# Latent attention: both heads' gate products in front of the next pair's query rotation on VectorE

## The reference

```
q = einsum('bsr,rhd->bshd', q_c, w_uq)          # 128 plain + 64 rotary features a head
q_rope = apply_rope(q[..., 128:], cos, sin)
q_lat = einsum('bshd,rhd->bshr', q[..., :128], w_uk)
s = q_lat . kv_c + q_rope . k_rope              # times ATTN_SCALE, masked by chunks of 64
o_lat = softmax(s) . kv_c
o = einsum('bshr,rhd->bshd', o_lat, w_uv)
return (o * silu(z)) @ w_out                    # z: the gate, 2048 features of the input projection
```

## Time and profile before

| | us |
| --- | --- |
| median of 3 runs | 2120.88 |
| lowest and highest run | 2120.36, 2125.22 |
| span of the profiled execution, first to last instruction | 2123.0 |
| PE busy | 1988.0 |
| DVE busy | 1021.4 |
| ACT busy | 852.1 |
| POOL busy | 797.5 |
| stretch of the eight pairs of heads, about | 1704 to 2015 |

### The profile page before, as it was taken

One profiled execution on the slowest core, in us unless ns is written; L12 is line 12 of the kernel. 1 busy time (PEld: TensorE's weight loads), 2 busy tenths in 40 slices (PEclk: granted clock), 3 DMA queues, 4 the chain that ended last, 5 costly groups with the idle time before them and its releaser, 6 DMA issues.

```text
span 2123.0 us, 29194 instructions
## 1 busy us (share of the span) xinstructions
PE 1988.0 (94%) x9640; PEld 1642.4 (77%) x9640; DVE 1021.4 (48%) x2371; ACT 852.1 (40%) x1566; POOL 797.5 (38%) x368
## 2 busy tenths in 40 slices
PE   7889999999999899999999998999999889999896
PEld 5778788888778788878888886877887567777684
DVE  5483765421254767546553216657312664444414
ACT  4463422222343676542222224222223465555523
POOL 3323454444454100126444442545444223242340
PEclk9889999999999899999999999999999989999999
DMA  7432455422333112126553322322322112121121
GB/s 244 127 92 67 150 178 164 138 92 96 99 110 121 36 45 66 42 79 199 176 168 99 99 95 74 106 92 95 99 93 95 43 57 69 40 69 49 60 79 40
DMA packets 70011, 209.40 MB, mean 99 GB/s; under 512 B 9739, under 2 KB 15115, under 8 KB 69948
## 3 DMA queue, kind: packets, MB, share of 16 engines
q1 hardware_dynamic: 57724, 174.72, 25.7%
q10 hardware_dynamic: 12224, 33.85, 5.0%
HBM read 196.90 MB, written 8.49 MB: 97 GB/s over the span
## 4 chain that ended last, share of the span: by engine, by line
PE 58%; issue 21%; DVE 9%; POOL 9%; ACT 2%; DVEq 0%; POOLq 0%; ACTq 0%
PE bank L938 15%; PE bank L939 15%; PE bank L940 15%; POOL wsp L442 9%; PE bank L1215 3%; PE bank L1362 1%; PE bank L1199 1%; PE bank L1381 1%; PE bank L1188 1%; PE bank L1084 1%; PE bank L1373 1%; PE bank L1211 1%; PE bank L972 1%; PE bank L1061 1%; DVE gen L1614 0%
## 5 line engine op out<-in xcount | busy, mean ns | idle before, releaser
L442 POOL TENSOR_TENSOR wsp<-raw,wsp 128x1024 fp32r<-128x1024 f32 x294 | 730.6, 2490 | 1047.9 <-ACT wsp L515 1047.7
L938 PE MATMUL bank<-xs,wsp 128*128 128x512 f32 x1320 | 525.9, 398 | 36.0 <-DVE mid L2040 16.0
L939 PE MATMUL bank<-xs,wsp 128*128 128x512 f32 x1320 | 519.1, 393 | 0.0
L940 PE MATMUL bank<-xs,wsp 128*128 128x512 f32 x1320 | 518.9, 393 | 0.0
L515 ACT ACTIVATE wsp<-raw 128x1024 fp32r<-128x1024 f32 x294 | 307.3, 1052 | 234.4 <-PE bank L940 205.6
L938 PEld LDWEIGHTS bank<-xs,wsp 128*128 128x128 f32 x1320 | 251.3, 190 | 97.0 <-issue 32.3
L938 PE MATMUL bank<-xk,wsp 128*128 128x512 f32 x752 | 295.4, 393 | 9.5 <-DVE xk L1482 5.1
L939 PE MATMUL bank<-xk,wsp 128*128 128x512 f32 x752 | 294.5, 392 | 0.0
L940 PE MATMUL bank<-xk,wsp 128*128 128x512 f32 x752 | 294.4, 391 | 0.0
L940 PEld LDWEIGHTS bank<-xs,wsp 128*128 128x128 f32 x1320 | 250.8, 190 | 53.6
L939 PEld LDWEIGHTS bank<-xs,wsp 128*128 128x128 f32 x1320 | 251.4, 190 | 52.1 <-issue 1.4
(11 more groups left out here) (287 smaller groups left out, 2548.3 us busy)
## 6 DMA issues: line engine op xcount, KB each, us to landing
raw<-weights SPq DMA_DIRECT2D x294, 512.0 KB, 3.3
gen<-ada ACTq DMA_DIRECT2D x48, 512.0 KB, 3.7
tmp<-mid SPq DMA_DIRECT2D x64, 128.0 KB, 2.9
bias_b<-bias_row ACTq DMA_DIRECT2D x1, 4096.0 KB, 37.5
mid<-bias_b SPq DMA_DIRECT2D x8, 512.0 KB, 3.8
hT<-xT SPq DMA_DIRECT2D x2, 1024.0 KB, 10.3
bias_a<-bias_row ACTq DMA_DIRECT2D x1, 2048.0 KB, 16.9
mid<-bias_a SPq DMA_DIRECT2D x8, 256.0 KB, 2.9
```

Of the source, the lines that this page charges most:

```text
L442: pool.tensor_tensor(wsp[:, slot, 1, :], raw[:, slot, :], wsp[:, slot, 0, :].bitcast(F32), ALU.subtract).then_inc(w_ready, 1)
L938: pe.matmul(dst, w[0], x[0], start=first, stop=False)
L939: pe.matmul(dst, w[0], x[1], start=False, stop=False)
L940: return pe.matmul(dst, w[1], x[0], start=False, stop=last)
```

## The change

Both gate products of a pair now stand next to each other, and the rotation of the next pair's queries comes after the second. The last pair has no rotation. Nothing else is altered: the same instructions, waits and semaphores.

```
                     dve.tensor_tensor(mid[:, hp * 2 + e, :], bank[6 + e][:, :], zs[e], ALU.mult).then_inc(mid_ready, 1)
-                    if not last and e == 0:
-                        rotate(hp + 1, hp * RING + (u0 + 2))
+                if not last:
+                    rotate(hp + 1, hp * RING + (u0 + 2))
```

## The result

| kernel | median, us | lowest to highest | ratio to before, 95% interval |
| --- | --- | --- | --- |
| before | 2122.32 (6 runs) | 2120.36 to 2125.22 | |
| changed | 2132.35 (6 runs) | 2128.80 to 2137.62 | 1.0044 [1.0026, 1.0063] |

The forecast was 2111.7 us, with a range of 2103.0 to 2119.5; the measured time lies outside and on the other side. The profiled execution of the changed kernel took 2132.33 us and has a span of 2130.6, 7.6 more than before. The part in front of the pairs is the same program and came out shorter in this execution (first product of pair 0 at 1742.17 against 1744.69), so the pairs and what follows them lost 10.1 us.

The account below looks back on a forecast made before the run. The prediction saw TensorE idling 2.29 us per pair boundary for VectorE's second gate product; GpSimd's chain would then bound. Gains 4 x 2.0 + 3 x 0.4 = 9.2 us gave 2113.8 span, 2111.7 forecast median, range 2103 to 2119.5.

Parts of the forecast that it names:

- step 1: At each pair boundary, TensorE's 2.29 us gap before the next gate projection (z0) goes; z0 starts 2.45 us earlier.
- step 2: VectorE's rotation moves behind the second product, starting 0.68 us later; rotated queries just in time, no new wait for scores.
- step 3: First block's exponential waits for ScalarE's second split, so it starts 1.47 us earlier instead of 2.45.
- step 4: VectorE's first normalisation meets GpSimd's split B, is let in at its end, and ends about 1795.0, 0.25 us later.
- B: GpSimd's second weight split; also the rival: first normalisation not held into that split, 23.2 us gained, 2097.7, chance 0.12.
- C: GpSimd's third weight split; also the rival: clock falls as often, later, among the scores; -2.8 us, 2118.1, chance 0.17.
- A: GpSimd's first weight split in a pair, queued behind two rope subtractions.
- Step 5: Split C follows B without pause and holds the second normalisation; third maximum 0.39 us earlier at a full-clock boundary.
- D: Rival: held VectorE instruction enters only when GpSimd's queue is dry; seven clock falls, +14 us, 2134.9, chance 0.07.

Follow-up runs that it names:

- before_c_late: Kernel before, with ScalarE's half of split C moved to the end of the softmax: 2124.55 us, ratio 0.9997.
- a_early: Changed kernel, with split A done before the rotated queries on both ScalarE and GpSimd: 2101.00 us, ratio 0.9910 to before.
- a_early_c_late: Changed kernel, with split A before the rotated queries and ScalarE's half of split C at the end of the softmax: 2100.26 us, ratio 0.9917 to before.
- c_late: Changed kernel, with ScalarE's half of split C moved from behind block 0's exponential to the end of the softmax: 2107.72 us, ratio 0.9938 to before.
- fourth: Changed kernel, with a needless 128x512 GpSimd product back to back behind split C: 2145.31 us, ratio 1.0110 to before.
- act_norm0: Changed kernel, with block 0 normalised by ScalarE instead of VectorE, behind its half of split C: 2106.51 us, ratio 0.9943 to before.
- act_pause: Changed kernel, with a needless 0.6 us ScalarE copy ahead of its half of split B in each pair: 2118.54 us, ratio 0.9984 to before.
- pause_fourth2: Changed kernel, with a needless ScalarE copy ahead of split B and a needless GpSimd product behind split C: 2118.03 us, ratio 0.9980 to before.

## Why the prediction was wrong
**The gap (step 1)** was right: TensorE's wait for L2040 is gone, z0 follows at 0.23 us and at full clock.

**The rotation (step 2)** was right but for a bit: it starts 1.40 us after the first product instead of 0.61, +0.79 in place of +0.68, and the scores wait 0.20 us for it.

**The exponential (step 3)** was right: ScalarE's second split sets it, 4.60 us behind the first rope subtraction (forecast 4.69).

**The failed step is step 4**: "then it falls into B, which runs to 1794.20 + 0.68 = 1794.88", and that it would be let in at the end of B. From the first rope subtraction I forecast the end of the first normalisation at about 7.4 us (1795.0 - 1787.59); measured 9.67 (1795.55 - 1785.88), the end of C. The earlier trace rows was one case, and it is a true case of the other kind: A is there the first instruction of a run, begun after 6.40 us of idling, and at each of the seven boundaries B is the second or later. Pair 0 repeats it in every kernel here in which VectorE normalises block 0 (1.92 to 1.93 us). I noted that the end of everything queued was the other bound and gave it 0.07; the one row at hand did not match the case in what turned out to decide, whether the running split had begun from a pause.

**Step 5** failed in two ways. The second normalisation isn't held at all, since the first comes out of its hold only behind C. And the 1.69 us that it took in the kernel before had no price: before_c_late takes it away and gains nothing. I had seen VectorE's maximum start 0.06 us after the normalisation's end and not that TensorE's scores for it (L1365) ended at that very time.

**The rivals.** D had the mechanism: the first normalisation ends with C, 9.79 us forecast, 9.67 measured. Its price at a full-clock boundary, +1.33 us, was near: where the clock did not fall, VectorE's first product of the next boundary came 37.77 us after this one's (1781.08 to 1818.85), and 36.59 before (1782.91 to 1819.50), +1.18. It had forecast seven clock falls, and there are six. It came out at +14 and the median moved by +10.0; the profiled execution divides as follows. The six full turns took 225.9 us before and 232.8 now, +6.8; six times 1.18 is 7.1, so the clock's falls cost about as much now (five of these turns, 6.1 us) as before (four, 6.4 us). The last turn took 33.97 and now 36.73, +2.8: the hold and a clock fall that it did not have. The tail has the remaining 0.5. B's full gain of 23 us is nearly reached by a_early and a_early_c_late (20 to 21 below the kernel before in their series), once the hold ends early. C was not the case: clocks did fall among the scores, but behind the long wait, and where the wait is shorter (c_late, a_early) they hardly fall.

## What to carry to other kernels
When work is moved away from a VectorE wait, look at which GpSimd instructions it will then meet, and whether these run back to back: here a held SBUF-to-SBUF VectorE instruction cost the rest of the run, not the rest of one instruction, unless the instruction that it met was the first of its run. So when a change fills a gap, ask what used the gap as a separator: here the 2.29 us on TensorE had kept the first normalisation behind A and B. Where a row is taken as the precedent for a hold, check that it agrees in what stood ahead of it, too, and before a long instruction is called "on the path" look whether another releaser of its successor ends at the same time.

## What the runs showed of the hardware
- A VectorE instruction from SBUF to SBUF (a normalisation of 128 or 256 columns, an addition with two SBUF inputs) stood still while GpSimd subtracted: 4.40 us instead of 0.28 with the rest of B and all of C ahead of it, 5.64 with one more instruction behind C, while maxima that read PSUM, reciprocals and one-column operations kept their times (0.29, 0.16, 0.15 us).
- It is let in at the end of the running GpSimd instruction when this is the first of a run (after a pause of 0.35 us or more in the pairs, of 0.03 us early in the program, or after VectorE has just been let in), and otherwise only at the end of the run. In the changed kernel, fourth and act_norm0 21 of 21 boundaries follow this, in a_early, act_pause and pause_fourth2 all holds too. Why the chip does so stays open: no run here looks inside. The Trainium skill has the clash (Advanced Engine Details and Errata, Mode Summary: GpSimd and two-port VectorE instructions block each other); that section doesn't say for how long. The traces agree in both directions. In the pairs of heads only VectorE was seen to pay: GpSimd's splits took 2.34 to 2.41 us there in the kernel before, whether an instruction stood waiting or not. Outside the pairs GpSimd pays too: a split that began at 250.42 beside a VectorE instruction of 128x1024 from SBUF to SBUF (249.94 to 251.56) took 3.40 us.
- 0.6 us of added work on ScalarE in each pair made the changed kernel 14 us faster (2132.35 to 2118.54).
